# Fourier mixing with half the products woven into the value projection, and a changed order of vector work where sums join x

## The reference

```python
u = h @ w_in[l]                                 # q, k, v, glu_in, four_in
fc = four_in.astype(jnp.float32).reshape(b, s, N_GROUPS_C, GROUP_C)   # 256 tokens, 4 groups of 128 channels
fr = jnp.fft.fft2(fc, axes=(1, 3), norm='ortho').real.astype(x.dtype)
y_c = fr.reshape(b, s, WIDTH_C) @ w_proj_c[l]
gates = jax.nn.sigmoid(h @ w_gate[l] + b_gate[l]).reshape(b, s, N_BRANCH, d)
x = x + merged @ w_out[l]
h2 = rmsnorm(x, norm2_g[l])
```

## Time and profile before

| | |
|---|---|
| median of 3 runs | 1243.1 us (1242.74 to 1243.14) |
| the profiled execution's own time | 1242.84 us |
| its span, first to last instruction | 1241.5 us |
| PE busy | 1236.1 us |
| DVE, ACT, POOL busy | 954.6, 722.9, 439.3 us |
| DMA queue q1 | 232.67 MB, 53.5% of 16 engines' span |
| granted TensorE clock | 1.00 over the span |

### The profile page before, as it was taken

The page is one execution under the profiler, slowest core; times in us unless marked ns, Lnnn a source line. Parts: engine busy times, 40 slices in busy tenths (PEclk is TensorE's granted clock), DMA queues, the critical chain, the costliest instruction groups (busy, mean ns, idle before and its releaser), DMA issues.

```text
span 1241.5 us, 17116 instructions
## 1 busy us (share of the span) xinstructions
PE 1236.1 (100%) x6638; PEld 1055.3 (85%) x6638; DVE 954.6 (77%) x1389; ACT 722.9 (58%) x1024; POOL 439.3 (35%) x354
## 2 busy tenths in 40 slices
PE   9999999999999999999999999999999999999999
PEld 8987788888888889888888888888988888888887
DVE  6865667677787478985878888976898587888895
ACT  7755545377775365577836555546457674655552
POOL 0011231039882079377420112008747750012100
PEclk9999999999999999999999999999999999999999
DMA  9753335555555448644554554465865454555442
GB/s 360 274 197 136 136 119 172 194 187 178 203 176 197 169 170 278 204 160 174 177 211 170 189 184 166 173 223 185 285 181 197 148 175 164 204 183 191 160 164 117
DMA packets 39007, 233.74 MB, mean 188 GB/s; under 512 B 4752, under 2 KB 5392, under 8 KB 13072
## 3 DMA queue, kind: packets, MB, share of 16 engines
q1 hardware_dynamic: 38928, 232.67, 53.5%
HBM read 225.31 MB, written 1.05 MB: 182 GB/s over the span
## 4 chain that ended last, share of the span: by engine, by line
PE 98%; DVE 1%; DMA 0%; ACT 0%; SPq 0%; issue 0%
PE ps L656 19%; PE ps L563 18%; PE ps L565 18%; PE ps L564 18%; PE ps L661 10%; PE ps L568 5%; PE ps L582 2%; PE ps L624 1%; PE ps L623 1%; PE ps L622 1%; PE ps L724 1%; PE ps L1212 1%; DMA raw<-in_w 0%; PE ps L894 0%; PE ps L809 0%; PE ps L810 0%
## 5 line engine op out<-in xcount | busy, mean ns | idle before, releaser
L1302 ACT ACTIVATE whi<-raw 128x2048 fp32r<-128x2048 f32 (+1 forms) x212 | 400.2, 1891 | 117.2 <-PE ps L565 105.2
L2074 DVE TENSOR_TENSOR wlo<-raw,whi 128x2048 fp32r<-128x2048 f32 x168 | 388.2, 2316 | 89.4 <-ACT whi L1302 88.4
L1900 POOL TENSOR_TENSOR wlo<-raw,whi 128x512 fp32r<-128x512 f32 x176 | 229.1, 1336 | 88.5 <-ACT whi L1302 85.5
L656 PE MATMUL ps<-hh,whi 128*128 128x512 f32 x1056 | 255.9, 392 | 0.9 <-DVE x L2522 0.9
L656 PEld LDWEIGHTS ps<-hh,whi 128*128 128x128 f32 x1056 | 192.9, 188 | 37.7 <-ACT whi L1302 1.3
L563 PE MATMUL ps<-whi,hh 128*128 128x512 f32 (+1 forms) x504 | 200.8, 398 | 0.0
L565 PE MATMUL ps<-whi,hh 128*128 128x512 f32 (+1 forms) x504 | 195.4, 388 | 0.0
L564 PE MATMUL ps<-wlo,hh 128*128 128x512 f32 (+1 forms) x504 | 195.1, 387 | 0.0
L1872 POOL TENSOR_TENSOR st<-st,sm 128x1 f32<-128x1 f32 (+2 forms) x28 | 45.1, 1609 | 309.5 <-DVE st L2128 229.3
L661 PEld LDWEIGHTS ps<-hh,wlo 128*128 128x128 f32 x1056 | 137.8, 191 | 6.7
L661 PE MATMUL ps<-hh,wlo 128*128 128x256 f32 x1056 | 139.8, 282 | 0.0
(11 more groups left out here) (347 smaller groups left out, 2063.7 us busy)
## 6 DMA issues: line engine op xcount, KB each, us to landing
raw<-in_w SPq DMA_DIRECT2D x202, 1024.0 KB, 4.9
raw<-in_w SPq DMA_DIRECT2D x12, 256.0 KB, 6.4
gain<-in_bias SPq DMA_DIRECT2D x12, 256.0 KB, 5.1
kst<-kh SPq DMA_DIRECT2D x16, 128.0 KB, 2.9
qst<-qh SPq DMA_DIRECT2D x16, 128.0 KB, 2.3
raw<-in_w SPq DMA_DIRECT2D x2, 560.0 KB, 11.2
x<-in_x SPq DMA_DIRECT2D x4, 256.0 KB, 6.2
gain<-in_rows SPq DMA_DIRECT2D x2, 512.0 KB, 5.7
```

What stands on the lines that cost most here:

```text
L656: pe.op.matmul(o[:, :], wh[:, k, c], t.hh[:, k, :, :], start=k == 0, stop=False, skip_group_check=True)
L1302: act.op.activation(t.whi[i % NHI][:, c], t.raw[i % NRAW][:, c], ACT.Copy).then_inc(*at("act_hi", ("hi", i)))
L1900: pool.op.tensor_tensor(t.wlo[i % NRAW][:, half(k)], t.raw[i % NRAW][:, half(k)], t.whi[i % NHI][:, half(k)].bitcast(F32), ALU.subtract).t ...
L2074: dve.op.tensor_tensor(t.wlo[i % NRAW][:, c], t.raw[i % NRAW][:, c], t.whi[i % NHI][:, c].bitcast(F32), ALU.subtract).then_inc(*at("dve_lo ...
```

## The change

1. The tokens' transform uses that cosines and sines of even and odd frequencies are even or odd about the middle. DVE folds the halves, `xf[0]` becomes their sum and `xf[1]` their difference, and each is multiplied by a table of 128 columns in place of 256. The channels' transform makes only cosine products and sine products; DVE forms `fr` from them by a difference and a mirrored sum (`mirrored`), with the sine products copied to SBUF by ACT first (`sines`).
2. This part stands inside v's unit: 3 steps of v, the tokens' products of groups 0 and 1, 2 steps, four products, 2 steps, four products, 1 step. The rounding of v (tt 1) and the seeds of the gate units on ACT stand behind it.
3. In `to_x`, DVE's chunk for the second up unit moves behind the last add and the last lower halves.
4. At the start, the first quarter of x is loaded from ACT's queue in place of SP's, and PE's warm-up matmuls are 22 and 17 in place of 28 and 34.

```diff
+BEFORE, BETWEEN = 3, (2, 2, 1)
...
-    load_x(0, 0)
...
-    warm(28)
+    warm(22)
     pe.wait_ge(*on("small"))
     first_turned(0, 0)
-    warm(34)
+    warm(17)
...
-        run(rows(f"v{l}", *h))
+        def over_tokens(g):
+            for tt in range(2):
+                pe.wait_ge(*on("free", (f"xf{l}", tt)))
+            pe.wait_ge(*on("cs", l))
+            pe.wait_ge(*on("T12", l, g - 2) if g >= 2 else on("free", ("q", l, "T", g)))
+            for odd in range(2):
+                product(t.sc[g % 2][:, odd * 128:odd * 128 + 128], t.xf[odd][:, g * 128:g * 128 + 128],
+                        t.csT[:, odd, :], names=[("fourier 1", l, g)] * odd)
+        def over_channels(k):
+            pe.wait_ge(*on("T12", l, k))
+            pe.wait_ge(*on("cd", l))
+            pe.wait_ge(*on("fr sums", l, k - 2) if k >= 2 else on("free", ("k", l, "T", 1 - k)))
+            o, T = (t.ob, t.tp)[k % 2], t.T12[k % 2]
+            product(o[:, 0:129], t.cdT[:, 0, :], T[:, 0:129])
+            product(o[:, 129:256], t.cdT[:, 1, :], T[:, 129:256], names=[("fourier 2", l, k)])
...
+        g = rows(f"v{l}", *h)
+        steps(g, BEFORE)
+        weave(fourier(), g)
+        run(g)
...
-        weave(chain(fourier(), attention(), after_attention()), back, 2)
+        weave(chain(attention(), after_attention()), back, 2)
...
+    act.op.dma_start(t.x[:, 0, half(0)], d["in_x"][tok(0), half(0)]).then_inc(*at("d_x0", ("x", "in", 0, 0), by=16))
...
+        first = copied_rows(f"xf{l}", lambda tt: t.xf[0][:, :])
+        run(rows(f"xf{l}", lambda tt: None if tt else first(0)))
...
+        for k in (3, 4, 5):
+            seed(k)
...
         add(0, 1)
         late_lower(norm, 1, 0)
-        splits(chunks[2] + AHEAD)
         norm_mean(norm, 0)
         add(1, 1)
         late_lower(norm, 0, 1)
         late_lower(norm, 1, 1)
+        splits(chunks[2] + AHEAD)
         splits(chunks[3] + AHEAD)
         late_wide(norm)
...
+            dve.op.tensor_tensor(t.xf[1][:, :], t.xf[0][:, :], bank(name)[:, :], ALU.subtract).then_inc(*at("dve_out"))
+            await_own("dve_out")
+            dve.op.tensor_tensor(t.xf[0][:, :], t.xf[0][:, :], bank(name)[:, :], ALU.add).then_inc(
+                *at("dve_out", ("free", name)))
...
+            dve.op.tensor_tensor(f[:, 0:129], o[:, 0:129], t.sines[k % 2][:, :], ALU.subtract).then_inc(*at("dve_out"))
+            dve.op.tensor_tensor(f[:, 129:256], o[:, 127:0:-1], t.sines[k % 2][:, 127:0:-1], ALU.add).then_inc(
+                *at("dve_out", ("fr sums", l, k)))
...
+            for p in range(2):
+                for k in (2 * p, 2 * p + 1):
+                    mirrored(k)
+                conv_some(3)
+                for k in (2 * p, 2 * p + 1):
+                    fourier_lower(k)
+                yield BETWEEN[p + 1]
```

More of the change, by code:

```diff
@@ L404, in place @@
     t.T12 = [at(f"T12{i}", y + 10 + 2 * i, [128, S]) for i in range(2)]
-    t.csT = at("csT", y + 14, [128, 2, S])
-    t.cdT = at("cdT", y + 18, [128, 3, 128])
+    t.csT = at("csT", y + 14, [128, 2, 128])
+    t.cdT = at("cdT", y + 18, [128, 2, 128])
+    t.fr = [at(f"fr{i}", y + 11 + 2 * i, [128, S]) for i in range(2)]
+    t.sines = [at(f"sines{i}", y + (15, 15.5625)[i], [128, 129]) for i in range(2)]
     t.E2 = [at(f"E2{i}", y + 2 * i, [128, S]) for i in range(2)]
@@ L1177, in layer @@
         qk_turned("q")
-        run(rows(f"v{l}", *h))
-        def fourier():
[L1181 to L1200, removed]
@@ L1202, in attention @@
+        def fourier():
+            for g in (0, 1):
+                over_tokens(g)
+            yield BETWEEN[0]
+            for k in (0, 1):
+                over_channels(k)
+            for g in (2, 3):
+                over_tokens(g)
+            yield BETWEEN[1]
+            for k in (2, 3):
+                over_channels(k)
+            yield BETWEEN[2]
+        g = rows(f"v{l}", *h)
+        steps(g, BEFORE)
+        weave(fourier(), g)
+        run(g)
         def attention():
@@ L1209, in attention @@
                     if tt == 0:
-                        pe.wait_ge(*on("WT", l, hd - 1) if hd else on("fr", l, 3))
+                        pe.wait_ge(*on("WT", l, hd - 1) if hd else on("fr sums", l, 3))
                     for k in range(2):
@@ L1218, in attention @@
                     if hd == 0:
-                        pe.wait_ge(*on("fr", l, 3))
+                        pe.wait_ge(*on("fr sums", l, 3))
                     if hd == 4:
@@ L1780, in gate_out, with tokens_out, sines_out @@
             return out
-        def fourier():
[L1784 to L1795, removed]
+        def tokens_out(g):
+            act.wait_ge(*on("fourier 1", l, g))
+            if g >= 2:
+                act.wait_ge(*on("fourier 2", l, g - 2))
+            act.op.activation(t.T12[g % 2][:, :].rearrange("p (m o) -> p m o", o=2),
+                              t.sc[g % 2][:, 0:S].rearrange("p (o m) -> p m o", o=2), ACT.Copy).then_inc(
+                *at("act_out", ("T12", l, g)))
+        def sines_out(k):
+            act.wait_ge(*on("fourier 2", l, k))
+            act.wait_ge(*(on("fr sums", l, k - 2) if k >= 2 else on("sines ends", l)))
+            act.op.activation(t.sines[k % 2][:, 1:128], (t.ob, t.tp)[k % 2][:, 129:256], ACT.Copy).then_inc(
+                *at("act_small", ("sines", l, k)))
+        def fourier():
+            for g in (0, 1):
+                tokens_out(g)
+            yield BETWEEN[0]
+            for k in (0, 1):
+                sines_out(k)
+            for g in (2, 3):
+                tokens_out(g)
+            for k in (0, 1):
+                upper(("fr hi", l, k), t.frh[:, k, :], t.fr[k][:, :], ("fr sums", l, k))
+            yield BETWEEN[1]
+            for k in (2, 3):
+                sines_out(k)
+            for k in (2, 3):
+                upper(("fr hi", l, k), t.frh[:, k, :], t.fr[k - 2][:, :], ("fr sums", l, k))
+            yield BETWEEN[2]
+        g = rows(f"v{l}", value_out(f"v{l}", lambda tt: t.v2[tt][:, :], []))
+        steps(g, BEFORE)
+        weave(fourier(), g)
+        run(g)
+        if l == 0:
+            act.wait_ge(*on("x", "f3", 1, 1))
+        for k in (3, 4, 5):
+            seed(k)
         lw = st[:, 128:160].rearrange("p (h t c) -> p h t c", h=8, t=2)
@@ L2751, in layer, with halves_folded @@
                 conv_some(4)
-        for _ in rows(f"xf{l}"):
+        def halves_folded(tt):
+            if tt == 0:
+                return
+            name = (f"xf{l}", 1)
+            dve.wait_ge(*on("free", (f"xf{l}", 0)))
+            dve.wait_ge(*on("got", *name))
+            dve.op.tensor_tensor(t.xf[1][:, :], t.xf[0][:, :], bank(name)[:, :], ALU.subtract).then_inc(*at("dve_out"))
+            await_own("dve_out")
+            dve.op.tensor_tensor(t.xf[0][:, :], t.xf[0][:, :], bank(name)[:, :], ALU.add).then_inc(
+                *at("dve_out", ("free", name)))
@@ L2753, in layer, with mirrored @@
+        for _ in rows(f"xf{l}", halves_folded):
             conv_some(2)
         qk_lower("q")
-        for _ in rows(f"v{l}", value_out(f"v{l}", t.v2[0][:, :], [])):
-            conv_some(2)
-        def fourier():
[L2759 to L2764, removed]
+        def mirrored(k):
+            o, f = (t.ob, t.tp)[k % 2], t.fr[k % 2]
+            dve.wait_ge(*on("sines", l, k))
+            dve.op.tensor_tensor(f[:, 0:129], o[:, 0:129], t.sines[k % 2][:, :], ALU.subtract).then_inc(*at("dve_out"))
+            dve.op.tensor_tensor(f[:, 129:256], o[:, 127:0:-1], t.sines[k % 2][:, 127:0:-1], ALU.add).then_inc(
+                *at("dve_out", ("fr sums", l, k)))
@@ new lines, in fourier_lower @@
+        def fourier_lower(k):
+            lower([("fr", l, k)], t.frl[:, k, :], t.fr[k % 2][:, :], t.frh[:, k, :], ("fr hi", l, k))
+        def fourier():
+            for i in range(2):
+                dve.op.memset(t.sines[i][:, 0:129:128], 0.0).then_inc(*at("dve_out", *([("sines ends", l)] * i)))
+            yield BETWEEN[0]
+            for p in range(2):
[5 more added lines that the diff above has]
+                yield BETWEEN[p + 1]
@@ L2766, in layer, with v_rows @@
+        def v_rows():
+            for _ in rows(f"v{l}", value_out(f"v{l}", t.v2[0][:, :], [])):
+                conv_some(2)
+                yield
+        g = v_rows()
+        steps(g, BEFORE)
+        weave(fourier(), g)
+        run(g)
+        conv_some(4)
         lw = st[:, 128:160].rearrange("p (h t c) -> p h t c", h=8, t=2)
@@ L2895, in programs @@
     pe_program(engines["pe"], t, ev, pb)
-    act_program(engines["act"], t, ev, pb)
+    act_program(engines["act"], t, ev, pb, d)
     dve_program(engines["dve"], t, ev, pb)
```

11 lines of the change are left out of this document (4 added, 7 removed).

## The result

The changed kernel takes 1247.2 us (median of 7, 1245.85 to 1248.71), the kernel before 1242.74 us (median of 7, 1242.42 to 1243.14). The ratio is 1.0037, with a 95% interval of 1.0027 to 1.0046: it is slower by 4.5 us, and its times scatter four times as widely. The profiled execution took 1247.2 us with a span of 1245.9 us, 4.4 us more than the span of before.

A forecast was written before the change was run, and what follows sets the result against it. PE's own work was taken to bound the kernel. Products −6.96, seed wait +6.54, to x +1.6 and start −0.4 gave +0.8 us on 1242.84, so 1243.6 us, with a range of 1238.8 to 1246.4.

The forecast's parts named there:

- Products: Fourier products on PE: fewer columns save 3.48 us per layer, −6.96 us in both, with nothing hiding it.
- The wait for the seed: End of v's unit: the first gate matmul waits for ACT's seed, 3.27 us per layer, +6.54 us in both.
- The walk through ACT, DVE and POOL: Step-by-step timing in v's unit: POOL's pieces delay DVE's `frl`, the first seed ends at 518.55, PE starts near 518.65.
- The floor: Least seed wait: v's second half is copied only behind v's last matmul; 0.2 + 0.5 + 0.6 given as 1.36 us per layer.
- To x: Where sums join x: the norm's copies come later, 1.3 us behind mo, 0.15 behind out0 and out1; together +1.6 us.
- Start: Kernel start: raw's first pieces are issued earlier and the clock may rise later; −0.4 us, from −0.6 to +1.5.
- The clock: PE's clock behind the seed's wait: no loss counted in the sum, since it stayed at 1.00 through waits up to 0.9 us.
- rival D: PE's wait for the seed drops PE to its lower clock level, so work behind runs at half rate; 1249.2 us, chance 0.10.
- A: Forecast case, whole kernel: time saved and given back; 1243.6 us, its ends 1241.6 to 1246, chance 0.58.
- Taps moved into attention: Ten DVE taps moved on into attention lie beside PE's gate units, counted 0; without that cover, 4.0 us per layer.
- The signs to look for: Profile after: PE busy about 7 us less, seed waits about 3.3 us twice, `xn` waits, slow `frl`, first projection 0.4 us earlier.

The follow-up runs named there:

- Experiments 5: Changed kernel with DVE's four taps ahead of the second mirrored pairs moved behind v: 1241.52 us.
- 6: Changed kernel with POOL writing zeros in place of the subtraction for the one weight chunk per layer made during v's unit: 1241.23 us.
- Experiment 1: Changed kernel with the first seed moved ahead of ACT's upper parts of the first two groups: 1240.94 us.
- experiment 3: Kernel before with only the move of DVE's chunk in the three places where sums join x: 1244.61 us.
- experiment 10: Kernel before with only the new start (x's first quarter from ACT's queue, 22 and 17 warm-up matmuls): 1242.91 us.
- experiment 4: Changed kernel with six extra unused products on PE between v's last matmul and the gate unit: 1243.76 us.
- experiment 2: Changed kernel with DVE's chunk for the second up unit put back ahead of the mean in all three places: 1244.65 us.

## Why the prediction was wrong

It said 1243.6 us, 1238.8 to 1246.4, and no measurable change as the likeliest. Measured are 1247.2 us. The step that failed is the clock, which the sum held at nothing; the other terms are off by less, and in part against each other.

- **Products, −6.96:** right. The three stretches in v's unit take 0.81, 1.70 and 0.80 us, and three returns to v cost 0.08 each: 3.55 us, as computed. One row was misread: the matmul at 519.09 is the gate unit's second, and the first stands at 518.77. The 0.23 that the prediction takes off is by chance the distance that belongs to it, and 7.03 us is the cost of the old block with its return of 0.09. In before PE wanted the seed at 518.77, 4.1 and not 4.4 us behind its end; nothing hangs on that.
- **The wait for the seed, +6.54:** right in its cause, a little too large: 2.93 us per layer for 3.27. The walk through ACT, DVE and POOL holds nearly row for row: mirrored pairs at 517.10 to 517.9 (forecast to end at 517.05 where v ends at 515.38; v's end stands at 516.61 here, 1.2 us on), the two `frl` 2.22 us under POOL. Experiments 5 and 6 each take one link out and get the time that follows from it (1241.5 us for 1241.0, 1241.2 for 1241.5). Experiment 1 takes the whole wait away, and 2.9 us come back at L1228. The floor's terms add up to 1.3, not 1.36.
- **To x, +1.6:** right, 1.85; experiment 3 measures 1.9. The places behind out0 and out1 cost 0.26 each and not 0.15.
- **Start, −0.4:** nothing that can be measured (experiment 10), where I had taken a gain.
- **The clock, 0: the step that failed.** The prediction had it as rival D, at a chance of 0.10 and outside the range, with this argument against it: "the clock stayed at 1.00 through the waits of up to 0.9 us". Those waits say nothing of one three times as long, and it said itself that none was as long. The Trainium skill ("TensorE: Matmul & The Clock Gate", section "Why this matters for your kernels"), which it named beside that, warned of the fall. The runs show the fall behind waits of 2.8 to 2.9 us: 3.2 us in the profiled execution, and 3.4 us between the changed kernel and the one whose wait is filled (experiment 4). With 3.2 the sum is 1243.6 + 3.2 = 1246.8. D's size was wrong too: I took 2.8 us per place from the start, where PE comes from rest; after a wait of 2.9 us it is 1.6, about 3.4 us at half rate. No row of before could give the price or the chance, but with a forecast wait of over 3 us the fall was no case for 0.10, and the range should have taken it in.
- **The range:** the bounds given for the terms add up to 1240.4 to 1247.8, not to A's 1241.6 to 1246. The upper end leaves out the start's +1.5. With it the range would have held 1247.2, and by luck, since the start cost nothing.
- **Taps moved into attention, 0:** right for the changed kernel, where PE's own delay covers them. The prediction named the price if the cover went (4.0 us per layer); with the seed's wait gone, 1.45 us per layer appeared (experiment 1), and four taps fewer removed them.

The miss of 3.6 us is then the clock's +3.2, −0.7 at the seed, +0.25 at the sums, +0.1 at the start and the 0.7 us that stays unassigned.

The signs to look for were named well except for one: PE's busy time fell by 3.9 and not 7 us, because matmuls at half rate count as busy for longer.

## What to carry to other kernels

Where the busiest engine never waits, a new wait has two prices: its length, and what the clock loses behind it. Waits of up to 1.3 us cost their length here; those of 2.9 us cost half as much again where the clock fell, which it did at least once in all 18 executions of the two kernels with such waits (the changed one and experiment 2). In an in-order program, ask of every moved block what used to stand in the middle of it: the seed stood between Fourier copies before and behind all of them after, and one line that puts the first of them back was worth 6.3 us. And remove one wait at a time: behind the first lay a second that it had covered.

## What the runs showed of the hardware

- Behind a wait of PE of 2.8 to 2.9 us the granted clock went to 0.50 for about 3.4 us, which cost 1.6 us. The fall came 1.2 us and 0.4 us behind the end of the wait in the two layers of the changed kernel, about 0.6 us before its end in layer 0 of experiment 2, and not at all in layer 1 of that execution.
- Waits of 1.2 and 1.3 us (by the view of waits) showed no fall in any of 33 executions of three kernels (experiments 3, 5 and 6), whose mean granted clock was 1.00. No run has a wait between 1.3 and 2.8 us.
- Extra matmuls of no use in the wait kept the clock at 1.00 in all 11 executions and made the kernel 3.4 us faster (experiment 4).
- Two DVE subtractions of 128x256 with both inputs in SBUF take 0.75 us alone and 2.22 us while POOL subtracts pieces of 128x512; a copy of 128x128 from SBUF to SBUF, 0.23 us by itself, takes 1.28 in the same company. With POOL writing zeros, and done before DVE's work began, the two subtractions took 0.75 us (experiment 6).
